# Layer-norm sums on VectorE, experts taken in an order set by their token counts, row-pair weight loads, and a rearranged start

## The reference, cut to what matters

```python
x = x + token_mixers(rmsnorm(x))     # 36 MB of projections, a gating unit, and a convolution:
    conv = causal depthwise conv, width 31, of glu, + conv_b
    y_b  = silu(layernorm(conv, g, b)) @ w_branch_b      # mean and variance over 1024 channels
    v_a  = layernorm(gelu(v_a))                          # per token, an output as well
x = x + moe(rmsnorm(x))
    logits = x @ w_router + b_router;  top 4 of 32 experts, softmax over the four
    gate, up = split(x @ w_up[e] + b_up[e])              # w_up[e]: 1024 x 2048, 8 MiB
    act = (clip(up) + 1) * (min(gate) * sigmoid(1.702 * min(gate)))
    y  += weight * (act @ w_down[e] + b_down[e])         # w_down[e]: 1024 x 1024, 4 MiB
y = rmsnorm(x)
```

## Time and profile before

| what | value |
|---|---|
| median of 3 runs | 1353.06 us (1351.2 to 1353.18) |
| profiled execution, its own time | 1346.7 us |
| its span | 1344.8 us |
| PE busy | 1195.9 us, 89% |
| DVE busy | 595.3 us, 44% |
| POOL busy | 460.8 us, 34% |
| ACT busy | 250.2 us, 19% |
| DMA moved | 448.96 MB, mean 334 GB/s over the span |

### The profile page before, as it was taken

The page is one execution under the profiler, slowest core; times in us unless marked ns, Lnnn a source line. Parts: engine busy times, 40 slices in busy tenths (PEclk is TensorE's granted clock), DMA queues, the critical chain, the costliest instruction groups (busy, mean ns, idle before and its releaser), DMA issues.

```text
span 1344.8 us, 30188 instructions
## 1 busy us (share of the span) xinstructions
PE 1195.9 (89%) x11163; PEld 589.0 (44%) x11164; DVE 595.3 (44%) x1251; ACT 250.2 (19%) x487; POOL 460.8 (34%) x797
## 2 busy tenths in 40 slices
PE   8999899999999988797799599879799898699996
PEld 7777677775544433232233233323233233233343
DVE  1999951321644433243344235324344243244444
ACT  2012122101222222111122112112122121112222
POOL 0012300000441445444444455444445454444440
PEclk9999999999899999898799899879899899799999
DMA  8983423334796899999999999999999999999981
GB/s 260 313 257 123 135 82 109 127 125 192 288 377 261 348 395 417 418 417 416 417 417 418 418 417 419 418 417 417 417 418 415 418 415 411 418 416 411 395 345 57
DMA packets 110953, 448.96 MB, mean 334 GB/s; under 512 B 8526, under 2 KB 42894, under 8 KB 78107
## 3 DMA queue, kind: packets, MB, share of 16 engines
q1 hardware_dynamic: 110062, 446.54, 83.9%
q10 hardware_dynamic: 813, 1.21, 0.3%
q0 software_dynamic: 48, 0.85, 0.1%
HBM read 447.00 MB, written 2.42 MB: 334 GB/s over the span
## 4 chain that ended last, share of the span: by engine, by line
PE 57%; DMA 12%; DVE 11%; issue 8%; POOL 6%; SPq 6%; ACT 0%; POOLq 0%; DVEq 0%
PE banks L1321 21%; PE banks L1331 12%; DMA ring<-in_w_down 10%; PE banks L1117 9%; DVE R L772 8%; POOL ring L502 6%; SPq L385 3%; PE banks L1097 3%; PE banks L1076 3%; PE banks L1040 3%; PE banks L1236 2%; DMA R<-in_w_spatial 1%; PE banks L1083 1%; SPq L333 1%; PE banks L1106 1%
## 5 line engine op out<-in xcount | busy, mean ns | idle before, releaser
L1321 PE MATMUL banks<-ring,hT 128*32 128x512 f32 x3328 | 440.7, 624 | 95.9 <-POOL ring L502 80.6
L502 POOL COPY ring<-big 128x512 f32<-128x512 f32 x248 | 143.4, 626 | 572.3 <-SPq L391 572.3
L502 POOL COPY ring<-R 128x512 f32<-128x512 f32 x496 | 288.3, 626 | 129.4 <-DMA R<-in_w_up 126.0
L310 DVE TENSOR_TENSOR xt<-xt,banks 128x1024 f32<-128x1024 f32 x106 | 128.8, 1216 | 433.2 <-PE banks L1097 433.2
L1331 PE MATMUL banks<-ring,hT 128*32 128x256 f32 x3328 | 233.0, 400 | 11.5 <-DMA ring<-in_w_down 10.0
L1321 PEld LDWEIGHTS banks<-ring,hT 128*32 128x32 f32 x3328 | 98.3, 112 | 232.1 <-POOL ring L502 104.6
L1331 PEld LDWEIGHTS banks<-ring,hT 128*32 128x32 f32 x3328 | 111.6, 116 | 199.2 <-issue 133.1
L1117 PE MATMUL banks<-hT,ring 128*128 128x288 f32 x768 | 189.8, 408 | 0.0
L1117 PEld LDWEIGHTS banks<-hT,ring 128*128 128x128 f32 x768 | 146.0, 191 | 39.9
L652 ACT COPY WT<-banks 128x256 f32<-128x256 f32 x52 | 19.4, 373 | 539.6 <-PE banks L1331 539.6
L772 DVE SCALAR_TENSOR_TENSOR R<-big,convw,R 128x256 f32<-128x256 f32 x240 | 107.4, 526 | 0.0
(11 more groups left out here) (226 smaller groups left out, 757.6 us busy)
## 6 DMA issues: line engine op xcount, KB each, us to landing
ring<-in_w_down SPq DMA_DIRECT2D x128, 1024.0 KB, 11.7
R<-in_w_up SPq DMA_DIRECT2D x124, 1024.0 KB, 18.3
ring<-in_w_up SPq DMA_DIRECT2D x70, 1024.0 KB, 9.4
big<-in_w_up SPq DMA_DIRECT2D x62, 1024.0 KB, 14.1
ring<-in_w_in SPq DMA_DIRECT2D x24, 1024.0 KB, 11.7
ring<-in_w_branch_b SPq DMA_DIRECT2D x4, 1024.0 KB, 4.9
ring<-in_w_branch_a SPq DMA_DIRECT2D x4, 1024.0 KB, 5.0
ring<-in_w_out SPq DMA_DIRECT2D x4, 1024.0 KB, 5.0
```

What stands on the lines that cost most here:

```text
L310: nc.vector.tensor_tensor(dst, dst, rows, ALU.add).then_inc(y_added, 1)
L502: ins = nc.gpsimd.tensor_copy(ring[:, k, h * 512:(h + 1) * 512], parked[k][:, h * 512:(h + 1) * 512])
L1321: ins = mm(UP[g * BLK:(g + 1) * BLK, :], xT[:, k, :], ring[:, k, g * 512:(g + 1) * 512], start=k == 0, stop=k == UP_SLOTS - 1)
```

## The change

Four edits in one.

1. **Mean and variance.** DVE adds the 8 chunks of the convolution into one (`tensor_reduce` over the chunks, into `tmpc[:, 0]`), and later those of the squares; PE then needs one matmul with `mean_w` each. The mean's matmul moves from after tile 17 to after tile 20, the variance's from after tile 23 to after tile 26. DVE subtracts the mean only after it has normalised v. ACT's square moves from tile n = 18 to n = 24, the root of the variance from n = 24 to n = 28.
2. **Experts' order.** Experts 0 and 1 stay at places 0 and 1. The others are ranked by count, and rank r goes to place 2 + (19 r + 29) mod 30, computed on DVE with a matmul in between. The numbers of blocks in order of place become 1 2 2 1 2 2 1 2 2 1 2 1 3 2 1 2 2 1 2 2 1 2 1 2 2 1 2 2 1 2 1 1; before they were 1 2 3 2 1 2 1 2 1 1 2 2 1 1 2 2 1 1 2 1 2 2 1 2 2 1 1 2 2 2 2 2. SP reads an expert's number for its place from `order`; `column` carries the place too.
3. **Row pairs.** A partition takes two neighbouring rows of `w_down`, one run of 8 KiB. To match, the transposes of the raw up-projection and of `b_up` read every second element.
4. **Beginning and pass.** Four of the eight vector loads move from ACT to SP, ahead of the first weight block. The copy of the cached rows waits until the GLU is done. Warm-up is 7 matmuls for 16, the vectors are turned between the first and second tile of x, and ACT's table of roots is loaded earlier. In a pass, `turn_rows` goes ahead of `combine_before`, whose sample part goes to the upper half of bank `DN`.

```diff
-for v, name in enumerate(vec_names):            # ACT: vector loads
+for v, name in enumerate(vec_names[0:4]):
+for v, name in enumerate(vec_names[4:8]):       # SP, ahead of load_block(0)
+    load(vecrows[(4 + v) * KC:(5 + v) * KC, :], ..., vec_in)
...
-                        "e (h p) n -> p (e h) n", p=P)
-                    dst = ring[:, k, :].rearrange("p (h n) -> p h n", h=2)
+                        "e (p h) n -> p (e h n)", p=P)
+                    dst = ring[:, k, :]
...
+            with sp.Fori(1, NE - 1) as place:
+                before = sp.value_load(items_before[0:1, bass.ds(place - 1, 1)], ...)
+                here = sp.value_load(order[0:1, bass.ds(place, 1)], ...)
+                after = sp.value_load(order[0:1, bass.ds(place + 1, 1)], ...)
...
+            dve.wait_ge(v_rows, 2 * KC)
+            dve.wait_ge(conv_done, KC)
+            V.tensor_reduce(tmpc[:, 0, :], conv.rearrange("p c t -> p t c"), AX.X, ALU.add).then_inc(conv_summed, 1)
...                                              # statistics of v, normalising v
+            dve.wait_ge(mean_ready, 1)
+            ins = V.tensor_tensor(conv, conv, bank[4][:, 0:T]..., ALU.subtract)
+            dve.wait_ge(sq_ready, 1)
+            V.tensor_reduce(tmpc[:, 1, :], sq.rearrange("p c t -> p t c"), AX.X, ALU.add).then_inc(conv_summed, 1)
...
-                if n == 2 * KC + 1:
-                    pe.wait_ge(conv_done, KC)
-                    for c2 in range(KC):
-                        ins = mm(bank[4][:, 0:T], mean_w[:], conv[:, c2, :], ...)
+                if n == 2 * KC + 4:
+                    pe.wait_ge(conv_summed, 1)
+                    mm(bank[4][:, 0:T], mean_w[:], tmpc[:, 0, :], start=True, stop=True).then_inc(mean_ready, 1)
-                if n == 3 * KC - 1:
-                    pe.wait_ge(sq_ready, 1)
-                    for c2 in range(KC): ...
+                if n == 3 * KC + 2:
+                    pe.wait_ge(conv_summed, 2)
+                    mm(bank[5][:, 0:T], mean_w[:], tmpc[:, 1, :], start=True, stop=True).then_inc(var_ready, 1)
...
+                pairs = raw.rearrange("t (b p h) -> t b h p", h=2, p=P)
                 for c in range(4):
-                    ins = tr(TB[:, c * P:(c + 1) * P], raw[:, c * P:(c + 1) * P])
+                    ins = tr(TB[:, c * P:(c + 1) * P], pairs[:, c // 2, c % 2])
...
-                combine_before(i, i + 2)
                 turn_rows(i + 1)
+                combine_before(i)
```

More of the change, by code:

```diff
@@ L46 @@
 MAX_ITEMS = NE + (T * TOPK) // BLK
-COLUMN_MAX = MAX_ROUNDS * NE - 1
+COLUMN_MAX = MAX_ROUNDS * NE * NE - 1
+FIXED = 2
+SPREAD = 19
 ROUND_BITS = 15 * NE
@@ L129, in hybrid_layer @@
         item_ids = sb("item_ids", [P, 1])
+        order = sb("order", [1, NE], I32)
+        key_bias = sb("key_bias", [NE, NE])
+        rank_at = sb("rank_at", [NE, NE - FIXED])
+        movable = sb("movable", [NE, 1])
+        first_place = sb("first_place", [NE, 1])
         big = sb("big", [P, KC * CB])
@@ L183, in hybrid_layer @@
         rankm = carve("prod", NT * NE).rearrange("p (t e) -> p t e", t=NT)
-        need = carve("prod", (MAX_ROUNDS - 1) * NE).rearrange("p (r e) -> p r e", e=NE)
-        ends_a, ends_b, started, begins = (carve("prod", NE) for _ in range(4))
-        item_expert, item_begin, item_column = (carve("prod", 1) for _ in range(3))
+        need = carve("prod", MAX_ROUNDS - 1, NE)
+        key_row, less = (carve("prod", NE, NE) for _ in range(2))
+        placed = carve("prod", 2 * NE, NE)
+        key_col, rank, place, blocks = (carve("prod", 1, NE) for _ in range(4))
+        ends, started, begins = (carve("prod", NE) for _ in range(3))
+        item_place, item_expert, item_begin, item_column = (carve("prod", 1) for _ in range(4))
         parked = (big[:, 0:SLOT], big[:, SLOT:2 * SLOT], R1[:, 0:SLOT], R2[:, 0:SLOT], R4[:, 0:SLOT], R3[:, 0:SLOT])
@@ new lines, in _ @@
+            link(V.tensor_scalar(less, key_row, key_col, None, ALU.is_lt))
+            V.tensor_reduce(blocks, need, AX.X, ALU.add)
+            link(V.tensor_reduce(rank, less, AX.X, ALU.add))
+            link(V.scalar_tensor_tensor(less[:, 0:NE - FIXED], rank_at[:], rank, slot_ids[0:NE, 0:NE - FIXED],
+                                        ALU.is_equal, ALU.mult))
+            link(V.tensor_reduce(place, less[:, 0:NE - FIXED], AX.X, ALU.add))
+            link(V.tensor_scalar(place, place, movable[:], first_place[:], ALU.mult, ALU.add))
@@ new lines, in _ @@
+            V.tensor_scalar(placed[:, 0:NE], slot_ids[0:NE, 0:NE], place, blocks, ALU.is_ge, ALU.mult)
+            V.tensor_scalar(placed[:, NE:2 * NE], slot_ids[0:NE, 0:NE], place, item_ids[0:NE, :], ALU.is_equal, ALU.mult
+                            ).then_inc(expert_placed, 1)
+            dve.wait_ge(order_summed, 1)
+            experts = bank[6][:, NE:2 * NE]
+            link(V.scalar_tensor_tensor(ends, bank[6][:, 0:NE], 1.0, slot_ids[:, 0:NE], ALU.add, ALU.add))
+            V.tensor_copy(order[:], experts[0:1, :])
@@ new lines, in _ @@
+            V.tensor_scalar(n_bodies[:], ends[0:1, NE - 1:NE], 1.0, None, ALU.subtract)
+            V.tensor_scalar(items_before[:], ends[0:1, :], 1.0, None, ALU.subtract).then_inc(before_known, 1)
+            take_x(0)
+            link(V.tensor_scalar(started, ends, item_ids[:, 0:1], None, ALU.is_le))
+            V.tensor_reduce(item_place, started, AX.X, ALU.add)
+            link(V.tensor_tensor(begins, ends, started, ALU.mult))
+            V.scalar_tensor_tensor(started, slot_ids[:, 0:NE], item_place, experts, ALU.is_equal, ALU.mult)
@@ L1190, in _ @@
                        WT[0:DS, :, 0:DS], start=True, stop=True).then_inc(ws_ready, 1)
-                if n == 3 * KC - 1:
-                    pe.wait_ge(sq_ready, 1)
-                    for c2 in range(KC):
-                        ins = mm(bank[5][:, 0:T], mean_w[:], sq[:, c2, :], start=c2 == 0, stop=c2 == KC - 1)
-                    ins.then_inc(var_ready, 1)
+                if n == 3 * KC + 2:
+                    pe.wait_ge(conv_summed, 2)
+                    mm(bank[5][:, 0:T], mean_w[:], tmpc[:, 1, :], start=True, stop=True).then_inc(var_ready, 1)
             pe.wait_ge(v_normed, NT)
@@ L1304, in _ @@
                 mm(DN[:, 0:NE], ones[:], mask[:, t2, :], start=t2 == 0, stop=False)
-            mm(DN[:, 0:NE], ones[0:NS, :], mask[0:NS, 2, :], start=False, stop=True).then_inc(counted, 1)
+            mm(DN[:, 0:NE], ones[0:NS, :], mask[0:NS, 2, :], start=False, stop=True)
+            for t2 in range(2):
+                mm(DN[0:NE, NE:NE + 1], mask[:, t2, :], ones[:, 0:1], start=t2 == 0, stop=False)
+            mm(DN[0:NE, NE:NE + 1], mask[0:NS, 2, :], ones[0:NS, 0:1], start=False, stop=True).then_inc(counted, 1)
             for tt in range(2):
@@ L1312, in _ @@
             gather_sample()
+            pe.wait_ge(expert_placed, 1)
+            mm(bank[6][:, 0:2 * NE], ones[0:NE, :], placed, start=True, stop=True).then_inc(order_summed, 1)
             keep_busy(3)
```

127 lines of the change are left out of this document (69 added, 58 removed).

## The result

The changed kernel took 1299.79 us (median, 1298.78 to 1300.47), beside 1352.83 us for the kernel before on the same chip: ratio 0.961, interval 0.9593 to 0.9626. It is faster by 53.0 us. The predicted time was 1302.5 us. The profiled execution took 1300.47 us (span 1298.5) where that of before took 1346.7: 46.2 us between the profiled ones, for 50.6 predicted.

What follows compares the result with a forecast made beforehand. The DMA stream was taken to bound the expert stage. Gains of 12.4 + 1.3 - 0.6 + 12.9 + 16.3 + 8.3 = 50.6 us, off a median of 1353.06, gave 1302.5 us, range 1289 to 1318.

Steps and rivals of the forecast that it cites:

- What bounds the kernel: Expert stage: the DMA stream bounds it at 417 GB/s, with idle time at both ends and a 19.3 us tail.
- Parts 1 and 1b: Mixing stage: sums on DVE gain 12.4 us; an earlier convolution start gains 1.3 us, bounds 0 and 3.
- The gap at tile 22: Mixing stage: PE waits 3 to 6 us for PSUM bank 2, held up by the late statistics of v.
- Part 2: Counts to the first item: PE waits for 11 DVE instructions; loss 0.6 us, bounds a 2 us gain and 1.5 loss.
- Parts 3 and 5: Expert stage's stream: new order cuts idle time, 12.9 us (6 to 18); 8 KiB runs gain 8.3 us (0 to 9).
- Part 4: End of the kernel: a one-item last expert shortens the tail behind the last byte; gain 16.3 us, bounds 12 and 18.
- The slow rival: Expert passes: strided transposes make the pass the bound, slower from 19.2 us per pass, 1373 us at 19.6; chance 3%.
- The sum: Whole kernel: all parts gain 50.6 us, taking the profiled execution from 1346.7 to 1296.1 us and the median to 1302.5.

Runs made afterwards that it cites:

- u_mean: The changed kernel with mean and variance summed by PE again, eight matmuls each at their old places; 1308.56 us, ratio 0.9691.
- u_copy: The changed kernel with POOL's copy of the cached rows issued at the start again; 1302.43 us, ratio 0.9642.
- u_order: The changed kernel with the experts in the order of their numbers, all new code still running; 1326.37 us, ratio 0.9823.
- x_tail: The changed kernel with movable experts one place earlier in the cycle, so an expert with two items comes last; 1310.83 us, ratio 0.9712.
- u_rows: The changed kernel with w_down read as before, two runs of 4 KiB per partition, and plain transposes; 1307.03 us, ratio 0.968.
- a_rows: The kernel before with the row pairs alone, runs of 8 KiB and transposes to match; 1343.25 us, ratio 0.9948.
- x_three: The changed kernel with the three-item expert at place 2 and a two-item one at place 12; 1299.77 us, ratio 0.9625.
- u_pass: The changed kernel with the old order within a pass, combine_before ahead of turn_rows; 1301.82 us, ratio 0.964.

## Why the prediction was right, point by point

**What bounds the kernel** was right. The stream is the bound, now more purely: 421 GB/s in nearly all of the stage, and PE still waits 57.4 us for POOL.

**Parts 1 and 1b** came out at 14.0 us for 13.7. The sum on DVE was taken at 4.4 us from the slope of the strided rows and took 4.2, 1.8 ns per element; the contiguous end, 2.7 us, would have been wrong. The gap at tile 22 is where it was foretold, at 2.2 us in this profile and up to 3.6 in others of the same code, for 3 to 6. The beginning was mis-sized: 1.3 us, measured 3.3 (`u_mean`) and 3.0 (`u_copy`). I had counted the copy's bytes at 300 GB/s against the convolution's start and taken back something for four loads. The copy costs more than its bytes: SP takes 3.6 us longer to issue. The sums are worth 10.6 us by the one pair of profiles and 10.2 to 13.0 by all, for 12.4. That the total fits to 0.3 us is luck, as single profiles differ by more.

**Part 2** was mis-sized: -3.2 us for -0.6. I gave the edit a gain if the busywork kept the clock up, and did not ask what more time at half would cost. The new steps themselves cost what I said: in `u_order` and `x_tail`, with the kernel before's 6.9 us at half clock, the stretch is 119.2 us for 118.5, a loss of 0.7. The other 2.5 us, and all 2.2 us of the seam (first `up` 5.89 us for 3.64), are the 10.2 us more at half clock in the changed kernel's profile. Why it lasted longer there than in `u_order`, whose code in this stretch is the same but for the table of the order, stays open.

**Parts 3 and 5**, the stream: 21.9 us for 21.2. The row pairs gave 8.1 to 9.2 us (`u_rows`), 8.3 predicted, and 6.1 alone (`a_rows`). The order gave 12.1 to 13.2 us (`u_order`), 12.9 predicted. The size was right, and one reason for it was wrong: I said that the hole of the expert with three items shrinks from 18 to 12 us at place 12, since the stream is behind by 6 us there. `x_three` puts it back to place 2, and the idle time is 20.5 us for 19.8. The window in the middle lacks 14.3 us, within my bounds of 8 to 18; the windows of the whole stage held 21.3 us of idle time for the 25.9 foretold, which had 2 us for wobble and 2.2 us for places 1 and 2 in it. Of the order's gain, 7.6 us are those near the end (`u_order`); the rest is at the start of the stage, and which of its neighbours makes the old order's start dearer stays open.

**Part 4**, the tail: 16.1 us for 16.3, with `u_order` (20.8) and `x_tail` (18.6) showing the item count of the last expert as the cause.

**The slow rival** was excluded: a pass with PE as the bound takes 15.76 us (starts at 728.38 and 744.14 us), for 16.04 before; 19.2 would have been needed. The 0.3 us less are the new order of a pass (`u_pass` has them back). Reading every second element makes weight loads longer, 186 ns for 141 in the mean, and the pass by 0.04 us at most (`u_rows`).

**The sum.** Profile against profile the gain was 46.2 us, 4.4 below my 50.6; 2.6 us of it are the routing and 2.2 us the seam, both nearly all half clock. That the forecast is still only 2.7 us off is luck with the offset: I carried over 6.4 us between profiled execution and median, and the changed kernel's profiled execution lies at its median (1300.47 and 1299.79). The two errors work against each other.

## What to carry to other kernels

Where a stream of loads bounds, write each shortfall as idle time (length times one minus its rate over the flat rate), count the tail behind the last byte apart, and order uneven work so that the smallest unit is last; the tail alone was a third of the gain here. A copy that nobody waits for still costs when it stands ahead of loads that somebody does. And where an edit lengthens a stretch of narrow matmuls, look for the granted clock there and put the price of half clock into the range: here 10.2 us more of it cost 4.7 us. Look at it in several profiles of the same code before putting it down to an edit.

## What the runs showed of the hardware that I had not expected

- In the same stretch of small matmuls and waits ahead of the first `up`, the time at half clock differed from profile to profile: 6.9, 13.7 or 17.1 us with matmuls of 32 columns as busywork, 3.4 and 6.9 with 128 columns. The stretch was 117.85 us long with the least of it and 121.65 with the 17.1, and a first `up` at half clock took up to 5.89 us for 3.64.
- A copy of 832 KB from memory to memory at the start lengthened SP's issue of four 1 MB loads from 5.99 to 9.57 us.
- Runs of 8 KiB in place of 4 KiB raised the sustained rate from 417 to 421 GB/s in a mixed stream, and gave 8.1 to 9.2 and 6.1 us of stream time in two kernels.
- Transposes that read every second element of float32 had weight loads of 186 and 185 ns in the mean, where plain ones had 141, in two pairs of kernels; in passes of 15.7 us it was hidden but for 0.04 us at most.
